# Six table transposes in place of eleven, and a first token tile that is loaded and squared in two halves

## What is computed

```python
def reference(x, w_in, lambda_q1, ..., t5_table, sinks, c_rel_table, ..., b_gate, ..., conv_w, conv_b, w_ffn_down):
    h = x
    u = rmsnorm(h, g_pre_mix[i])                       # 512 x 1024
    proj = u @ w_in[i]                                 # q, k, v of the branches A, B, C
    ya = diff_attention(..., t5_table[:, :A_HEADS], lam, lam_init, subln_g[i])
    yb = sliding_window_sink_attention(..., t5_table[:, A_HEADS:], sinks[i])
    yc = chunk_band_attention(..., c_rel_table[i])
    gates = jax.nn.sigmoid(u @ w_gate[i] + b_gate[i])
    h = h + rmsnorm(mixed @ w_out[i], g_post_mix[i])
    u = rmsnorm(h, g_pre_ffn[i])
    h = h + rmsnorm(conv_ffn(u, w_ffn_up[i], conv_w[i], conv_b[i], w_ffn_down[i]), g_post_ffn[i])
```

## Time and profile before

| | us |
|---|---|
| median of 3 runs | 841.32 (840.88, 841.32, 843.56) |
| the profiled execution, its own time | 841.03 |
| its span | 839.2 |
| PE busy | 831.0 |
| DVE, ACT, POOL busy | 647.0, 478.9, 398.6 |
| DMA read and written | 97.05 MB and 13.42 MB |

### The profile page before, as it was taken

How to read it: one execution, slowest core, us unless ns; L and a number is a source line. 1 busy time by engine, 2 the same in 40 slices (tenths; PEclk the granted TensorE clock), 3 DMA queues, 4 the chain that set the end, 5 groups by cost and what they waited for, 6 DMA issues and landing times.

```text
span 839.2 us, 13423 instructions
## 1 busy us (share of the span) xinstructions
PE 831.0 (99%) x4701; PEld 727.0 (87%) x4701; DVE 647.0 (77%) x1263; ACT 478.9 (57%) x905; POOL 398.6 (47%) x511
## 2 busy tenths in 40 slices
PE   8999999999999999999999999999999999999997
PEld 7888888888888888999998899899999999988885
DVE  6577777788776867966544389988888888999995
ACT  5475656777776664544443447556565656545662
POOL 6454434433352346986677426766565656010002
PEclk9999999999999999999999999999999999999999
DMA  7632133232223212334336631555554443396584
GB/s 238 175 102 73 53 100 100 75 99 57 82 80 69 80 44 82 114 114 120 95 101 218 201 134 52 187 174 170 170 171 118 121 119 121 132 312 242 170 285 157
DMA packets 138071, 111.35 MB, mean 133 GB/s; under 512 B 7607, under 2 KB 121215, under 8 KB 136724
## 3 DMA queue, kind: packets, MB, share of 16 engines
q1 hardware_dynamic: 136378, 102.05, 40.0%
q0 software_dynamic: 720, 5.24, 1.8%
q10 hardware_dynamic: 906, 3.20, 1.1%
HBM read 97.05 MB, written 13.42 MB: 132 GB/s over the span
## 4 chain that ended last, share of the span: by engine, by line
PE 97%; DVE 1%; DMA 0%; ACT 0%; issue 0%; POOL 0%; DVEq 0%; POOLq 0%
PE banks L2324 24%; PE banks L2326 24%; PE banks L2325 24%; PE banks L2626 3%; PE banks L2625 3%; PE banks L2624 3%; PE banks L2498 2%; PE banks L2407 2%; PE banks L2406 2%; PE banks L2794 1%; PE banks L2793 1%; PE banks L2795 1%; PE banks L2508 1%; PE banks L2470 1%; PE banks L2477 1%; PE banks L2342 1%
## 5 line engine op out<-in xcount | busy, mean ns | idle before, releaser
L871 POOL TENSOR_TENSOR ring_lo<-ring_raw,ring_hi 128x256 fp32r<-128x256 f32 x376 | 305.5, 846 | 278.1 <-ACT ring_hi L1036 277.8
L2324 PE MATMUL banks<-u_hi,ring_hi 128*128 128x512 f32 (+1 forms) x580 | 222.0, 383 | 0.0
L2326 PE MATMUL banks<-u_hi,ring_lo 128*128 128x512 f32 (+1 forms) x580 | 217.4, 375 | 0.0
L2325 PE MATMUL banks<-u_lo,ring_hi 128*128 128x512 f32 (+1 forms) x580 | 217.1, 374 | 0.0
L2326 PEld LDWEIGHTS banks<-u_hi,ring_lo 128*128 128x128 f32 x580 | 109.2, 188 | 20.0
L2325 PEld LDWEIGHTS banks<-u_lo,ring_hi 128*128 128x128 f32 x580 | 109.5, 189 | 18.1
L2324 PEld LDWEIGHTS banks<-u_hi,ring_hi 128*128 128x128 f32 x580 | 109.3, 188 | 17.8
L1036 ACT CAST ring_hi<-ring_raw 128x1024 fp32r<-128x1024 f32 x95 | 99.0, 1043 | 38.7 <-PE banks L2326 22.9
L2145 DVE SCALAR_TENSOR_TENSOR wide<-banks,cols,wide 128x511 f32<-128x511 f32 x88 | 64.6, 744 | 3.5 <-ACT wide L1402 1.6
L2324 PE MATMUL banks<-pages,ring_hi 128*128 128x512 f32 (+1 forms) x180 | 61.2, 340 | 0.0
L2325 PE MATMUL banks<-pages,ring_hi 128*128 128x512 f32 (+1 forms) x180 | 61.2, 340 | 0.0
(11 more groups left out here) (339 smaller groups left out, 2004.7 us busy)
## 6 DMA issues: line engine op xcount, KB each, us to landing
ring_raw<-in_w_ffn_up_dram SPq DMA_DIRECT2D x88, 256.0 KB, 3.5
ring_raw<-in_w_in_dram SPq DMA_DIRECT2D x59, 256.0 KB, 3.4
ring_raw<-in_w_ffn_down_dram SPq DMA_DIRECT2D x55, 256.0 KB, 3.7
ring_raw<-in_w_gate_dram SPq DMA_DIRECT2D x48, 256.0 KB, 3.3
split_tokens<-pages SPq DMA_DIRECT2D x5, 1024.0 KB, 7.0
pages<-split_tokens POOLq DMA_DIRECT2D x5, 1024.0 KB, 6.6
ring_raw<-in_w_out_dram SPq DMA_DIRECT2D x16, 256.0 KB, 3.1
second_tokens<-wide SPq DMA_DIRECT2D x10, 384.0 KB, 3.9
```

Source lines behind the costliest of these rows:

```text
L871: last = pool.tensor_tensor(wlo[:, r, c], raw[:, r, c], whi[:, r, c].bitcast(F32), ALU.subtract)
L2324: pe.matmul(out, lhs_hi, rhs_hi, start=start, stop=False)
L2325: pe.matmul(out, lhs_hi, rhs_lo, start=False, stop=False)
L2326: return pe.matmul(out, lhs_lo, rhs_hi, start=False, stop=stop)
```

## The change

Tables: `conv_w` and `conv_b` (four blocks of 44 rows of 128) and `b_gate` (24 rows of 128) are laid out as two blocks of 88 and 112 rows, and `c_rel_table` as two blocks of 128 rows and one of 64. So PE does six transposes in place of eleven. `load_small` issues seven loads for them in place of five. The loads that `sink` and `sub_raw` wait for now share a semaphore.

Tokens: tile 0 is loaded as two halves of 512 columns, each with its own semaphore. DVE squares the first half (512 columns) when it has landed, and then the last quarter (256 columns); ACT squares the third quarter (256 columns) in place of the first 512. DVE's fourth memset is moved from before the squares to between the scaling of tile 2 and tile 3.

```diff
-        conv_in = wide[0:44, 0, :].rearrange("p (c n) -> p c n", c=4)
+        taps_in, rest_in = wide[0:88, 0, 0:P], wide[0:112, 0, P:2 * P]
-        crel_in = wide[0:64, 1, 64:64 + 40].rearrange("p (a h) -> p a h", h=8)
-        bgate_in = wide[0:24, 1, 128:256]
+        crel_in = wide[:, 1, 64:64 + 24].rearrange("p (a h) -> p a h", h=8)
...
-            load_x(0)
+            sp.dma_start(x_tok[:, 0, 0:512], x_rows[0][:, 0:512]).then_inc(x_first, 16)
+            sp.dma_start(x_tok[:, 0, 512:1024], x_rows[0][:, 512:1024]).then_inc(x_loaded[0], 16)
             load_x(1)
...
-                sp.dma_start(crel_in, c_rel_table[0].rearrange("(a p) h -> p a h", p=64)).then_inc(small_loaded[3], 16)
-                sp.dma_start(conv_in[:, 0:3, :], conv_w[0].rearrange("c (j n) -> j c n", n=P)).then_inc(small_loaded[3], 16)
-                sp.dma_start(conv_in[:, 3, :], conv_b[0].rearrange("(j n) -> j n", n=P)).then_inc(small_loaded[3], 16)
-                sp.dma_start(bgate_in, b_gate[0].rearrange("(j n) -> j n", n=P)).then_inc(small_loaded[3], 16)
+                sp.dma_start(crel_in[:, 0:2, :], c_rel_table[0][0:2 * P].rearrange("(a p) h -> p a h", p=P))\
+                  .then_inc(small_loaded[3], 16)
+                sp.dma_start(crel_in[0:64, 2, :], c_rel_table[0][2 * P:2 * P + 64]).then_inc(small_loaded[3], 16)
+                sp.dma_start(taps_in, conv_w[0][0:2].rearrange("c (j n) -> (c j) n", n=P)).then_inc(small_loaded[3], 16)
+                sp.dma_start(rest_in[0:44], conv_w[0][2].rearrange("(j n) -> j n", n=P)).then_inc(small_loaded[3], 16)
+                sp.dma_start(rest_in[44:88], conv_b[0].rearrange("(j n) -> j n", n=P)).then_inc(small_loaded[3], 16)
+                sp.dma_start(rest_in[88:112], b_gate[0].rearrange("(j n) -> j n", n=P)).then_inc(small_loaded[3], 16)
...
                 if c == 1:
-                    pool.wait_ge(first_square, 1)
+                    pool.wait_ge(first_square, 2)
...
             act.wait_ge(x_loaded[0], 16)
-            square(0, 0, x_tok[:, 0, 0:512], 512)
+            square(0, 0, x_tok[:, 0, 512:768], 256)
...
-            dve.memset(pages[0:CHUNK, Q_LO_PG:Q_LO_PG + 2, :].bitcast(F32), 0.0).then_inc(q_lo_cleared, 1)
+            dve.wait_ge(x_first, 16)
+            dve.tensor_tensor_reduce(tmp[:, 0:512], x_tok[:, 0, 0:512], x_tok[:, 0, 0:512], 1.0 / D, EPS,
+                                     ALU.mult, ALU.add, norm_ms[:, 0, 3:4]).then_inc(first_square, 1)
             dve.wait_ge(x_loaded[0], 16)
-            dve.tensor_tensor_reduce(tmp[:, 0:512], x_tok[:, 0, 512:1024], x_tok[:, 0, 512:1024], 1.0 / D, EPS,
-                                     ALU.mult, ALU.add, norm_ms[:, 0, 0:1]).then_inc(first_square, 1)
+            dve.wait_ge(first_square, 1)
+            dve.tensor_tensor_reduce(tmp[:, 512:768], x_tok[:, 0, 768:1024], x_tok[:, 0, 768:1024], 1.0 / D,
+                                     norm_ms[:, 0, 3:4], ALU.mult, ALU.add, norm_ms[:, 0, 0:1]).then_inc(first_square, 1)
...
             u_low(1, 0)
-            for t in (2, 3):
-                xs(0, t, x_tok[:, t, :], spread_gain())
+            xs(0, 2, x_tok[:, 2, :], spread_gain())
+            dve.memset(pages[0:CHUNK, Q_LO_PG:Q_LO_PG + 2, :].bitcast(F32), 0.0).then_inc(q_lo_cleared, 1)
+            xs(0, 3, x_tok[:, 3, :], spread_gain())
...
-                pe.wait_ge(small_loaded[3], 5 * 16)
+                pe.wait_ge(small_loaded[3], 7 * 16)
                 pe.transpose(psum[0:12, O_BANK, 0:32], t5_in, ident[0:32, 0:32])
-                for c in range(4):
-                    pe.transpose(psum[:, O_BANK, 32 + 44 * c:76 + 44 * c], conv_in[:, c, :], ident[0:44, 0:44])
-                pe.transpose(psum[:, O_BANK, 208:232], bgate_in, ident[0:24, 0:24])
-                for a in range(5):
-                    last = pe.transpose(psum[0:8, O_BANK + 1, 64 * a:64 * a + 64], crel_in[:, a, :], ident[0:64, 0:64])
+                pe.transpose(psum[:, O_BANK, 32:120], taps_in, ident[0:88, 0:88])
+                pe.transpose(psum[:, O_BANK, 120:232], rest_in, ident[0:112, 0:112])
+                for a, n in enumerate((P, P, 64)):
+                    last = pe.transpose(psum[0:8, O_BANK + 1, P * a:P * a + n], crel_in[0:n, a, :], ident[0:n, 0:n])
                 last.then_inc(tables_turned, 1)
```

More of the change, by code:

```diff
@@ L461, in build_encoder @@
         x_loaded = [sem(f"x_loaded{t}") for t in range(TT)]
-        small_loaded = [sem(f"small_loaded{i}") for i in range(5)]
+        small_loaded = [sem(f"small_loaded{i}") for i in range(4)]
         raw_loaded = [sem(f"raw_loaded{r}") for r in range(RING)]
@@ L472, in build_encoder @@
         first_raw = sem("first_raw")
+        x_first = sem("x_first")
         first_square = sem("first_square")
@@ L642, in load_small @@
                 sp.dma_start(t5_in, t5_table).then_inc(small_loaded[3], 16)
-                sp.dma_start(crel_in, c_rel_table[0].rearrange("(a p) h -> p a h", p=64)).then_inc(small_loaded[3], 16)
-                sp.dma_start(conv_in[:, 0:3, :], conv_w[0].rearrange("c (j n) -> j c n", n=P)).then_inc(small_loaded[3], 16)
-                sp.dma_start(conv_in[:, 3, :], conv_b[0].rearrange("(j n) -> j n", n=P)).then_inc(small_loaded[3], 16)
-                sp.dma_start(bgate_in, b_gate[0].rearrange("(j n) -> j n", n=P)).then_inc(small_loaded[3], 16)
+                sp.dma_start(crel_in[:, 0:2, :], c_rel_table[0][0:2 * P].rearrange("(a p) h -> p a h", p=P))\
[5 more added lines that the diff above has]
+                sp.dma_start(rest_in[88:112], b_gate[0].rearrange("(j n) -> j n", n=P)).then_inc(small_loaded[3], 16)
                 for i, v in enumerate((lambda_q1, lambda_k1, lambda_q2, lambda_k2)):
-                    sp.dma_start(lam_in[:, i, :], v[0].partition_broadcast(P)).then_inc(small_loaded[4], 16)
-                sp.dma_start(sink[:], sinks[0].partition_broadcast(P)).then_inc(small_loaded[1], 16)
+                    sp.dma_start(lam_in[:, i, :], v[0].partition_broadcast(P)).then_inc(small_loaded[1], 16)
+                sp.dma_start(sink[:], sinks[0].partition_broadcast(P)).then_inc(small_loaded[0], 16)
                 sp.dma_start(sub_raw[:], subln_g[0].rearrange("(n a) -> n a", a=1)).then_inc(small_loaded[0], 16)
@@ L1620, in _ @@
             dve.wait_ge(x_loaded[2], 16)
-            dve.wait_ge(first_square, 1)
+            dve.wait_ge(first_square, 2)
             dve.tensor_tensor_reduce(tmp, x_tok[:, 2, :], x_tok[:, 2, :], 1.0, 0.0, ALU.mult, ALU.add,
@@ L1637, in tables @@
                    .then_inc(tables_out, 1)
-                dve.wait_ge(small_loaded[4], 64)
+                dve.wait_ge(small_loaded[1], 64)
                 for i in range(2):
@@ L1654, in tables @@
                 dve.tensor_scalar(neg_lam[:], lam_dif[:], -LAM_INIT, None, ALU.add).then_inc(lam_done, 1)
-                dve.wait_ge(small_loaded[0], 16)
+                dve.wait_ge(small_loaded[0], 2 * 16)
                 dve.tensor_scalar(sub_col[:], sub_raw[:], 1.0 - LAM_INIT, None, ALU.mult).then_inc(lam_done, 1)
-                dve.wait_ge(small_loaded[1], 16)
                 dve.tensor_scalar(neg_sink[:], sink[:], -1.0, None, ALU.mult).then_inc(lam_done, 1)
```

## The result

The changed kernel is slower: 843.16 us against 840.99, the medians of 22 runs each; the ratio is 1.0021 with a 95% interval of 1.0014 to 1.0029. The prediction was 840.6 with a range of 839.8 to 841.9. The move, 0.21%, is under the 0.3% that it named, but it goes the other way and the time lies 1.3 above the range.

What follows compares the result with a forecast made beforehand. The prediction took PE to bound the kernel, busy for 99% of the span. From the profiled 841.03 us it took 0.40 for the table transposes and 0.0 for the rest, giving 840.6, range 839.8 to 841.9.

Steps and rivals of the forecast that it cites:

- What bounds the kernel: Whole kernel: PE, busy 99% of the span; only time taken from PE's line or its waits counts.
- where the start is held: PE's turn of tile 2 at 14.91: held by tile 1's chain, PE's own line within 0.06; earlier tile 0 worth 0.
- the new squares: Tile 0's squares at the start: ACT's smaller piece makes the factor ready 0.21 sooner, worth 0 at the end.
- Tile 0's price: Loads at the start: tile 1 is issued 0.43 later by the split, cost taken as 0, bounds -0.05 and +0.43.
- Rival 2: Start: tile 1 lands later by the extra issue, 0.37 against the 0.40 saved, time 841.0; chance 0.12.
- The tables: PE's table transposes at 21.16: six take 0.64 where eleven took 1.04, saving 0.40, perhaps 0.05 more from drains.
- Their loads: SP's table loads: last issued at about 14.8, wanted at 20.8, hidden; cost 0, from 0 to 0.1.
- The memset: DVE at 14.86: the moved memset of 0.91 fits in an idle 1.73, cost 0.
- rival 5: At 14.86: the memset holds POOL and delays tile 3's turn, +0.62 less 0.40, time 841.25; chance 0.05.
- Rival 4: Tile 0's load: the first half lands no sooner than the whole, +0.23 against the 0.40, time 840.9; chance 0.07.
- rival 3: Table transposes: six cost what eleven did, time 841.0; chance 0.08.
- rival 1: Start: tile 1 too lands 0.2 sooner, so 0.21 comes on top, time 840.4; chance 0.10.

Runs made afterwards that it cites:

- after_again: The changed kernel unaltered, run again for a second trace: 842.87 us.
- after_again_2: The changed kernel unaltered, run a third time for another trace: 842.29 us.
- halves_only: The changed kernel with the old tables (eleven transposes, five loads), so only the token part and moved memset: 842.22 us, ratio 1.0017 to the kernel before.
- after_one_load: The changed kernel with token tile 0 in one load, squares, memset and tables as changed: 841.31 us, ratio 1.0008 to the kernel before.
- split_cols_2: The kernel before with tile 0 in two loads of 512 columns; ACT squares the second half, waiting for that alone: 842.43 us against 841.34.
- extra_load: The kernel before with one unused load of 128 4-byte values between tiles 0 and 1 on SP: 843.10 us, ratio 1.0027.
- tables_only: The kernel before with only the table part (six transposes, seven small loads), tile 0 as before: 841.22 us against 841.16.
- split_rows: The kernel before with tile 0 in two loads of 64 partitions with whole rows, both waited for before the squares: 843.58 us, ratio 1.0028.
- gap_only: The kernel before with no further load, SP waiting for GpSimd's identity between issuing tiles 0 and 1: 841.77 us against 841.30.
- after_hold: The changed kernel with SP issuing the weight loads only when tile 0 has landed whole: 842.80 us against 841.15 for the kernel before.
- tables_order: tables_only with the 64-row transpose moved to second place: 840.70 us against 841.15 for the kernel before, ratio 0.9997.
- start_late: The kernel before with SP waiting for DVE's first memset ahead of its first load: 841.99 us, ratio 1.0013.
- extra_after_tile1: The kernel before with an unused load of 128 4-byte values behind tile 1 on SP: 841.69 us, ratio 1.0003.
- split_cols: The kernel before with tile 0 in two loads of 512 columns, both waited for before the squares: 842.47 us, ratio 1.0017.

## Why the prediction was wrong

**What bounds the kernel, and where the start is held: right.** The chain behind the turn of tile 2 is tile 1's landing, ACT's square, POOL's factor and five quarters, POOL's factor of tile 2, DVE's scaling. A late tile 1 moved every link by the same: +1.25 at ACT and POOL, +1.24 at PE. It came to PE by the second way too that the prediction had within 0.06: PE's own line was 1.12 late from the turn of tile 1 on. And tile 0, ready 0.68 sooner at DVE (5.98 against 6.66), was worth nothing. Of the 0.68, 0.59 is the earlier landing, which is luck of the execution; from the landing to DVE's scaling it took 1.78 against 1.87, and 1.72, 1.91 and 1.66 in after_again, after_again_2 and halves_only. So the new squares gave between nothing and 0.21, where 0.21 was forecast. The three-piece squares cost a little more than said: DVE's 256 columns took 0.49, not 0.35, and waited 0.15 for the first piece's sum; POOL waits for that, not for ACT. DVE then idled 0.38 for PE's gain rows before the second half. All of it is hidden.

**Tile 0's price: the step that failed.** I wrote that tile 1's bytes are queued behind tile 0's until 4.0, long after its new issue, and took 0 for the split, with +0.43 as the upper bound. That term is what made the forecast wrong: in the three traces of the changed kernel the turn of tile 2 is 1.24, 1.69 and 1.48 late. Rival 2 had the right place and sign, a chance of 0.12, and a price of 0.37; the three traces of the changed kernel show tile 1 squared 1.25, 1.70 and 1.49 later than before (whose 6.08 is the latest of five traces with whole loads and tile 1 issued at once). The error was to price an added load by its issue on SP alone, and to treat the queues as a pipe whose rate doesn't depend on what is in it. The rows of before couldn't show the price, since no load stands there between tiles 0 and 1; one issue was then no upper bound. What I should have taken from those rows is that the start has no slack against tile 1 at all (I had 0.06).

What the runs put in its place has two parts. The rate is lower in most: 369 GB/s before and 370 in after_one_load, against 266, 337 and 253 in the three traces of the changed kernel, 265 in split_cols_2 and 270 in extra_load. And weights get in ahead of tile 1. Landing comes some 0.8 behind the bytes, an estimate from tile 0 in before; at 0.8 before the square of tile 1 the core had moved 1.07 MB before, 1.05 in tables_only and 1.02 in after_one_load, which is the two token tiles (1.05), but 1.28, 1.63 and 1.29 MB in after, 1.23 in split_cols_2 and 1.42 in split_rows. So tile 1 wasn't complete though more than its bytes had gone through. The share of the two parts differs: extra_load (270 GB/s, 1.06 MB) is the rate alone, and the latest landing of the changed kernel, in after_again, came at a rate that gap_only has too (337) but with 1.63 MB through. The wait for tile 1 is for a count of 16; the Trainium skill ("DMA: Bandwidth & Descriptors", "Two DMAs through the same engine are not ordered") says that nothing orders loads across the sixteen, which is in line with this. What makes the rate fall, and whether single engines lag, is not shown: the profile has no row by engine. It takes a further load on SP's own queue (the same half from ACT's queue left 371 GB/s). For tile 1 to be late this must stand ahead of it or within it; behind it, the rate falls later and tile 2 is late. A large load isn't needed (extra_load), nor small packets (split_rows), nor weights in flight (after_hold, 324 GB/s before 5.0 against 403).

**The tables: mechanism right, size off.** 0.40 was forecast and 0.22 came, as the 64-row transpose waits 0.22 behind the 128-row ones. I had taken the drain as a possible gain of 0.05, by counting steps and not looking at their order. In the order of tables_order the forecast's 0.64 for six is met (0.63). Their loads were hidden, as said, though the last was issued at 15.22 and not by 14.8; and PE wanted them at 21.16 or later, not at 20.8, since the tables are themselves what was to get shorter.

**The memset: right.** Hidden in DVE's wait. POOL's quarters beside it weren't held: three in 2.14 from 14.75, as before from 13.50, so rival 5 is out. Rival 4 is out as the first half landed 0.7 sooner than the whole, rival 3 as the tables took 0.81 and not 1.04, rival 1 as no trace has the turn of tile 2 before 14.9.

**The sum.** The start in the three traces is 1.0 to 1.5 late behind the tables. The spans without the late wait are 1.3 and 1.6 longer than before; the medians differ by 2.2. The 0.6 or more between them isn't settled. Seven of the 22 runs of after took longer than the slowest of its three profiled executions (843.68), and no trace shows what these lost. The wait near 790 (1.2, in one of three traces of the changed kernel) would give it if a late start made it more frequent: three of eight late starts had it and none of ten others. Against this, nine of start_late's eleven runs lie within 0.6 of each other, and DVE's idle time for the down weights is no longer in the other late starts. It stays open.

## What to carry to other kernels

A split of the first load buys an earlier start only for the chain that begins with it. Before splitting, find which load ends the wait of the engine that bounds the kernel some steps later. Price a further load ahead of it by a test with a tiny load in the same place, not by its issue time, and look at the next load behind as well. When small transposes of several row counts stand in the middle of full ones, sort them by rows, so that the row count changes as few times as can be; here that took 0.63 in place of 0.82 in the trace, and nothing that the time could show.

## What the runs showed of the hardware

- 512 bytes in a load of their own between two loads of 512 KB cost 1.95 us in the median of extra_load; the first 512 KB in two loads of 256 KB cost 1.1 in split_cols_2 (their intervals overlap). In the 1 us with the hole the core moved 140 to 156 GB/s in extra_load and 60 to 87 in extra_after_tile1, where before moves 344 to 426 from 3.5 to 6.5 us.
- With whole loads and tile 1 issued right behind tile 0, tile 1 was squared from 5.63 to 6.08 in five traces of different kernels; with tile 0 in two loads on SP, from 6.13 to 8.14 in eight.
- A second wait ahead of ACT's first activation moved its 1.28 us table load behind the wait, in split_cols and split_rows (it starts at 4.45 and 5.60 there, at 1.31 in before).
- A 64-row weight load waited 0.22 us behind 128-row transposes, in after and in tables_only.
